# The scaling of the compressed attention rows in block 1: four one-tensor operations in place of two tensor products

## What is computed

```python
s_c = jnp.einsum('bgrqd,bgnd->bgrqn', qb, k_c).astype(jnp.float32) * scale
p_c = masked_softmax(s_c, c_end[None, :] <= tpos[:, None])
o_c = jnp.einsum('bgrqn,bgnd->bgrqd', p_c.astype(dt), v_c)
...
return gb[..., 0:1] * o_c + gb[..., 1:2] * o_s + gb[..., 2:3] * o_w
```

## Time and profile before

| | us |
|---|---|
| median of 3 runs | 2785.0 |
| lowest, highest | 2784.23, 2790.51 |
| the profiled execution | 2787.24 |
| its span in the profile | 2785.4 |
| mean granted clock of PE over the span | 0.989 |
| PE busy | 2677.4 (96%) |
| DVE busy | 1566.4 (56%) |
| ACT busy | 1050.5 (38%) |
| POOL busy | 1178.7 (42%) |

### The profile page before, as it was taken

How to read it: one execution, slowest core, us unless ns; L and a number is a source line. 1 busy time by engine, 2 the same in 40 slices (tenths; PEclk the granted TensorE clock), 3 DMA queues, 4 the chain that set the end, 5 groups by cost and what they waited for, 6 DMA issues and landing times.

```text
span 2785.4 us, 38135 instructions
## 1 busy us (share of the span) xinstructions
PE 2677.4 (96%) x13128; PEld 2192.6 (79%) x13128; DVE 1566.4 (56%) x2514; ACT 1050.5 (38%) x1826; POOL 1178.7 (42%) x592
## 2 busy tenths in 40 slices
PE   7999888999999999999999999999899999999998
PEld 6877777778888878878887788888687778888886
DVE  7996766564342476476656735545623446653364
ACT  4225878623222254443324411112525553211133
POOL 3432595334444444364333344444442224444443
PEclk9999999999999999999999999999999999999999
DMA  3242000233222232221112322222231112332232
GB/s 134 91 149 85 16 24 9 68 129 100 98 98 92 96 131 84 80 95 61 54 39 96 133 98 98 92 97 98 91 103 60 46 46 91 128 98 91 98 98 91
DMA packets 67460, 242.89 MB, mean 87 GB/s; under 512 B 7771, under 2 KB 10116, under 8 KB 66572
## 3 DMA queue, kind: packets, MB, share of 16 engines
q1 hardware_dynamic: 59760, 215.37, 23.4%
q10 hardware_dynamic: 7580, 25.91, 2.6%
HBM read 232.80 MB, written 6.35 MB: 86 GB/s over the span
## 4 chain that ended last, share of the span: by engine, by line
issue 50%; PE 29%; POOL 18%; ACT 1%; DVE 1%; POOLq 1%; DVEq 0%; ACTq 0%
POOL w_lo L448 14%; PE bank L2596 7%; PE bank L2598 7%; PE bank L2597 7%; POOL stat L475 3%; PE bank L3146 2%; PE bank L3135 2%; POOL stat L472 2%; PE bank L2811 1%; POOLq L452 0%; PE bank L2782 0%; PE bank L3119 0%; ACT w_hi L595 0%; PE bank L3184 0%; PE bank L3185 0%
## 5 line engine op out<-in xcount | busy, mean ns | idle before, releaser
L448 POOL TENSOR_TENSOR w_lo<-raw,w_hi 128x1024 fp32r<-128x1024 f32 x398 | 972.8, 2444 | 1539.5 <-ACT w_hi L595 1418.3
L2596 PE MATMUL bank<-act,w_hi 128*128 128x512 f32 x3128 | 1259.2, 403 | 52.4 <-POOL w_lo L448 15.2
L2598 PE MATMUL bank<-act,w_lo 128*128 128x512 f32 x3128 | 1227.7, 392 | 0.0
L2597 PE MATMUL bank<-act,w_hi 128*128 128x512 f32 x3128 | 1226.3, 392 | 0.0
L595 ACT CAST w_hi<-raw 128x1024 fp32r<-128x1024 f32 x396 | 415.7, 1050 | 903.2 <-PE bank L2598 891.8
L2596 PEld LDWEIGHTS bank<-act,w_hi 128*128 128x128 f32 x3128 | 592.1, 189 | 199.9 <-issue 32.5
L2598 PEld LDWEIGHTS bank<-act,w_lo 128*128 128x128 f32 x3128 | 591.9, 189 | 127.2
L2597 PEld LDWEIGHTS bank<-act,w_hi 128*128 128x128 f32 x3128 | 593.2, 190 | 121.3 <-issue 5.5
L1691 DVE TENSOR_TENSOR X<-X,bank 128x512 f32 x56 | 38.5, 687 | 241.4 <-PE bank L2598 241.4
L2087 DVE CAST act<-tmp 128x512 f32 x64 | 142.6, 2228 | 10.0 <-DVE tmp L2083 5.2
L1843 DVE SCALAR_TENSOR_TENSOR bank<-big,cols,bank 128x512 f32<-128x512 f32 x174 | 117.0, 748 | 0.4
(11 more groups left out here) (428 smaller groups left out, 2944.1 us busy)
## 6 DMA issues: line engine op xcount, KB each, us to landing
raw<-in_w_dram SPq DMA_DIRECT2D x402, 512.0 KB, 3.4
act_f<-head_rows ACTq DMA_DIRECT2D x8, 768.0 KB, 4.2
proj_rows<-big ACTq DMA_DIRECT2D x4, 1024.0 KB
big<-proj_rows ACTq DMA_DIRECT2D x2, 2048.0 KB, 9.1
X<-in_x_dram SPq DMA_DIRECT2D x4, 512.0 KB, 7.6
act_f<-in_cw1k_dram ACTq DMA_DIRECT2D x4, 512.0 KB, 4.1
cst<-in_consts_dram ACTq DMA_DIRECT2D x2, 648.5 KB, 7.9
X<-big ACTq DMA_DIRECT2D x8, 128.0 KB, 3.6
```

The costliest lines, as they stand in the source:

```text
L448: pool.tensor_tensor(w_lo[:, u], raw[:, u].rearrange("p (k n) -> p k n", k=KT), w_hi[:, u].bitcast(F32), ALU.subtract).then_inc(w_lo_ready, 1)
L2596: pe.matmul(o, l_hi, r_hi, start=start, stop=False)
L2597: pe.matmul(o, l_hi, r_lo, start=False, stop=False)
L2598: return pe.matmul(o, l_lo, r_hi, start=False, stop=stop)
```

## The change

In `compressed_sum` the small product (four factors times four gates) and the large product (rows times factor, the factor spread over 31 columns) go. In their place come four tensor-scalar operations, one per token tile. Each reads 31 numbers per partition and multiplies them by the reciprocal and then by the gate, both given as one number per partition. `c_scaled` is raised by the last of the four. No wait stands between them.

```diff
                     link(v.tensor_reduce(to, rows, AX.X, ALU.add))
                     link(v.reciprocal(to, to))
-                    link(v.tensor_tensor(to, to, V_TOK[:, 4, :, h:h + 1].rearrange("p q a -> p (q a)"), ALU.mult))
-                    v.tensor_tensor(rows, rows, per_row(to), ALU.mult).then_inc(c_scaled, 1)
+                    for q in range(TT):
+                        ins = v.tensor_scalar(rows[:, q], rows[:, q], to[:, q:q + 1], V_TOK[:, 4, q, h:h + 1], ALU.mult, ALU.mult)
+                    ins.then_inc(c_scaled, 1)
```

## The result

The changed kernel takes 2803.4 us (median of 5 runs, 2796.5 to 2806.3), the kernel before 2785.0 (5 runs, 2784.1 to 2790.5). The ratio is 1.0053, 95% interval 1.0042 to 1.0064: slower by some 15 us where 12 were forecast. The two medians lie 18 us apart; both kernels scatter by 6 to 10 us in five runs, so the ratio with its interval is the better measure. The profiled execution took 2799.2 us, 12.0 above the profiled one of before. In a second group of runs the changed kernel took 2800.3 us and the kernel before 2789.1, ratio 1.0050 (1.0036 to 1.0064).

What follows compares the result with a forecast made beforehand. PE, busy 96% of the span, was taken to bound the kernel, waiting behind DVE's copy L1949. 9.2 us on the path plus 3.2 us of clock falls gave +12.4 us, 2797 us on the median of 2785.0; range 2783 to 2801.

Steps and rivals of the forecast that it cites:

- What bounds: Block 1's attention rounds: PE, busy 96% of the span, waits behind DVE copy L1949, 8.1 us in 7 waits.
- Order of the four: Four DVE operations at 0.20 us each replace two products; a sum without POOL goes from 0.92 to 1.32 us.
- Do they queue: Beside POOL's taps, the four one-tensor operations queue for POOL as the two products did, judged by nearest row L1861.
- Turns: Sums beside POOL: two operations per opening, then a whole hold of 0.75 us; 2.45 us against 1.61, +0.84 each.
- On the path: Share of the longer sums in block 1's rounds that PE waits for: 9.2 us together.
- term of the even heads: Five even heads' sums beside POOL: PE waits for the copy behind, so all counts, 4.2 us.
- that of the odd heads: Five odd heads' sums beside POOL: 0.24 us of slack taken off, 0.6 each, 3.0 us.
- six sums without POOL: Heads 0 to 3 and 14 at 0.4 us each, head 15 covered by ScalarE: 2.0 us.
- The clock: Longer PE waits in the rounds bring two more falls of the granted clock, 1.6 us of PE's work each: +3.2 us.
- B: Rival: the four queue but once begun run through, POOL's next claim coming behind them; +4.8 us, 2790 us; chance 0.2.
- C: Rival: one tensor read means no queueing, the 6.9 us of waits go; -1.2 us, 2784 us; chance 0.22.
- D: Rival: C with operations 0.13 us from start to start and one clock fall gone; 2779 us; chance 0.08.

Runs made afterwards that it cites:

- accumulator form: Changed kernel with each of the four operations also writing out its accumulator to a place nobody reads; 2787.0 us, 0.9994 of the kernel before.
- narrow taps: Kernel before and changed kernel, each with POOL's taps beside the rounds on 2 columns instead of 512; 2782.4 us (0.9977) and 2785.1 us (0.9987).

## Why the prediction came out as it did

- **What bounds.** That PE waits for the copy behind the sums was right: the waits doubled, and moving the sums took them and the time away, with the work unchanged.
- **Order of the four.** 0.207 us apart where 0.20 was taken, the sum 1.35 us where 1.32. The distance lies between the two bounds, 0.16 and 0.23, nearer to that of L1841, the form with two scalars.
- **Do they queue.** Right, and the accumulator form shows that a run of elements in SBUF is not enough by itself. The choice of L1861 as the nearest row held.
- **Turns.** 2.45 us per sum beside POOL forecast; the ten take 1.99 to 2.71, 2.53 in the mean. I had averaged over where in POOL's cycle a sum begins. In fact the four of every even sum began 0.2 to 0.3 us behind the start of POOL's add, so that the first operation was held long (it took 0.98 to 1.11 us) and the third for a short time (0.76); that is why the even sums scatter so little, 2.50 to 2.62.
- **On the path.** The total was near, the split was not. I had put +0.84 on even and odd sums alike. The even sums had been long before, 1.98 us in the mean with one of 3.05, and grew by 0.6 to 2.59; the odd ones, 1.26 before, grew by 1.2 to 2.48. So by the sum's own rule the term of the even heads was 3 us, not 4.2, and that of the odd heads 5 us, not 3.0. PE's waits at these ten places agree: they grew by 8.0 us, 3.0 at the even and 4.9 at the odd ones, where 7.2 were forecast. That 7.2 came so near to 8.0 is luck, two errors of opposite sign. The wait behind DVE's copy went from 8.1 to 19.1 us, well over the "12 us or more", since it took over the 3.0 us of ScalarE's. The 2.0 us of the six sums without POOL were not measured by themselves. With narrow taps all 16 sums, 0.43 us longer each, cost 2.8 us in all, less than half of their added order, so 2.0 for six of them was probably high.
- **The clock.** Two more falls were counted, +3.2 us. The profile has four in the rounds against two before, three of them behind even sums against one, as counted. The other one came behind a wait that had not changed (2.4 us near 303 us), and the one before at 488 us did not come again, so part of this agreement is luck as well. By the runs the share varies from 2 to 9 us; the median of the first five, 2803.4, lies above the range's end of 2801, while 1.0053 times 2785.0, 2799.8, lies inside.
- **Rivals.** B, no claim between the four, is out by the third operation's 760 ns. C and D needed that one-tensor operations don't queue. The accumulator form is what C described, and its time, which can't be told from that of the kernel before, fits C's -1.2 us.

## What to carry over

Several short DVE operations of this plain form, 0.2 us apart beside a busy GpSimd, cost one of its turns per pair, so count operations that contend, not elements: four of 31 columns were caught for longer than two of 4 and 124. Before making a step cheaper, look at what stands behind it in its engine's order: moving these sums by two or three rounds, in front of a stretch in which the engine waits anyway, gave the kernel before 9 us, and made the dear form as good as the cheap one. On an engine that is busy for half its time, place counts for more than price.

## What the runs showed of the hardware

A tensor-scalar of one element per partition was never held by POOL (128 of 128 at most 217 ns in the profiles before and after), one of 31 was (up to 1251 ns), and one of 31 that also writes its accumulator was not (64 of 64 under 308). In the order of DVE a tensor-scalar with two per-partition scalars on 31 elements costs 0.207 us, though each takes 0.29. And about equal waits of PE, of 2.0 to 2.4 us, are followed by a granted clock near 0.6 over 4 us in some places and executions and by 1.00 in others. The changed kernel, which has most of them, scattered over 10 us in its first five runs, the kernels with both sums moved over 4 in five or six runs each. That the waits make the scatter is likely and not shown.
